# Attention heads of a two-block model handled by the pair, and head norms of its recurrence taken per token, on one Trainium2 core

## What is computed

```
kk = heads(k * k_k)
kk = kk / jnp.maximum(jnp.sqrt(jnp.sum(kk * kk, axis=-1, keepdims=True)), 1e-12)
...
mean = jnp.mean(wkv, axis=-1, keepdims=True)
var = jnp.mean(jnp.square(wkv - mean), axis=-1, keepdims=True)
y = ((wkv - mean) * lax.rsqrt(var + GN_EPS)) * ln_w + ln_b
```

```
s = jnp.einsum('bqgrd,bkgd->bgrqk', qi, k).astype(jnp.float32) * scale
p = jax.nn.softmax(s, axis=-1).astype(v.dtype)
return jnp.einsum('bgrqk,bkgv->bqgrv', p, v)
```

## Time and profile before

| | |
|---|---|
| median of 3 runs | 2863.81 us (2863.75 to 2866.16) |
| profiled execution | 2862.11 us, of which the span is 2860.3 us |
| mean granted clock of TensorE | 0.966 |
| PE busy | 2600.9 us (91%) |
| DVE, ACT, POOL busy | 1240.2, 1085.9, 809.8 us (43, 38, 28%) |
| heads, layer 1 | from 2123.5 to 2335.6 us of the span |
| heads, layer 2 | from 2624.9 to 2789.5 us |
| rounds | from 471.2 to 1052.1 us |

### The profile page before, as it was taken

The page is one execution under the profiler, slowest core; times in us unless marked ns, Lnnn a source line. Parts: engine busy times, 40 slices in busy tenths (PEclk is TensorE's granted clock), DMA queues, the critical chain, the costliest instruction groups (busy, mean ns, idle before and its releaser), DMA issues. The chain is left out here.

```text
span 2860.3 us, 49221 instructions
## 1 busy us (share of the span) xinstructions
PE 2600.9 (91%) x19266; PEld 2041.7 (71%) x19266; DVE 1240.2 (43%) x1839; ACT 1085.9 (38%) x1682; POOL 809.8 (28%) x342
## 2 busy tenths in 40 slices
PE   8999979989898979888999999989978888998987
PEld 6887857868686857776778887767855566776665
DVE  3222024455655537344242220055846642584652
ACT  4443224343434323553233442233344422335441
POOL 3444433313232313112434444412210002232002
PEclk9999989999999989999999999999999999999998
DMA  4232322212121212111423233311110001121001
GB/s 135 90 95 92 105 66 86 91 52 83 59 83 59 83 39 74 52 38 59 134 82 95 88 95 98 100 37 53 55 41 1 1 9 51 52 74 59 1 1 66
DMA packets 52005, 188.49 MB, mean 66 GB/s; under 512 B 5760, under 2 KB 6016, under 8 KB 51712
## 3 DMA queue, kind: packets, MB, share of 16 engines
q1 hardware_dynamic: 50688, 181.74, 20.3%
q10 hardware_dynamic: 1152, 4.26, 0.4%
HBM read 183.88 MB, written 2.10 MB: 65 GB/s over the span
## 5 line engine op out<-in xcount | busy, mean ns | idle before, releaser
L2392 POOL TENSOR_TENSOR WLO<-RAW,WHI 128x1024 fp32r<-128x1024 f32 x334 | 804.7, 2409 | 2010.5 <-ACT WHI L299 2010.5
L299 ACT ACTIVATE WHI<-RAW 128x1024 fp32r<-128x1024 f32 x336 | 355.8, 1059 | 999.7 <-PE psum L313 708.8
L311 PE MATMUL psum<-HHI,WHI 128*128 128x512 f32 x872 | 353.8, 406 | 40.2 <-DVE HLO L397 15.0
L312 PE MATMUL psum<-HLO,WHI 128*128 128x512 f32 x872 | 347.0, 398 | 0.0
L313 PE MATMUL psum<-HHI,WLO 128*128 128x512 f32 x872 | 346.6, 397 | 0.0
L311 PE MATMUL psum<-H2HI,WHI 128*128 128x512 f32 (+1 forms) x536 | 197.3, 368 | 32.5 <-DVE H2LO L395 23.0
L311 PEld LDWEIGHTS psum<-HHI,WHI 128*128 128x128 f32 x872 | 165.8, 190 | 84.0 <-issue 43.9
L312 PEld LDWEIGHTS psum<-HLO,WHI 128*128 128x128 f32 x872 | 165.9, 190 | 41.7 <-issue 3.4
L313 PEld LDWEIGHTS psum<-HHI,WLO 128*128 128x128 f32 x872 | 165.7, 190 | 39.6
L312 PE MATMUL psum<-H2LO,WHI 128*128 128x512 f32 (+1 forms) x536 | 191.6, 357 | 0.0
L313 PE MATMUL psum<-H2HI,WLO 128*128 128x512 f32 (+1 forms) x536 | 191.2, 357 | 0.0
(11 more groups left out here) (394 smaller groups left out, 5196.6 us busy)
## 6 DMA issues: line engine op xcount, KB each, us to landing
RAW<-in_wstream SPq DMA_DIRECT2D x336, 512.0 KB, 3.5
X<-in_xT SPq DMA_DIRECT2D x8, 256.0 KB, 7.3
out_T<-OUT SPq DMA_DIRECT2D x4, 512.0 KB, 2.6
W3S<-in_lora ACTq DMA_DIRECT2D x5, 384.0 KB, 3.1
XC<-in_ctxT ACTq DMA_DIRECT2D x1, 1024.0 KB, 5.6
TRIG<-in_trig ACTq DMA_DIRECT2D x1, 960.0 KB, 7.6
FCC<-in_first SPq DMA_DIRECT2D x1, 576.0 KB, 9.0
LVL<-in_levels SPq DMA_DIRECT2D x1, 384.0 KB, 9.3
```

What stands on the lines that cost most here:

```text
L299: act.activation(WHI[:, q % 2, :], RAW[:, q % 2, :], ACT.Copy).then_inc(rounded, 1)
L311: pe.matmul(out, tile_of(WHI, slot, u), hi(kt), start=first and last[0], stop=False)
L312: pe.matmul(out, tile_of(WHI, slot, u), lo(kt), start=False, stop=False)
L2392: pool.tensor_tensor(WLO[:, s, :], RAW[:, s, :], WHI[:, s, :].bitcast(F32), ALU.subtract)\
```

## The change

**Heads.** A pair's two units are handled together. PE's order per pair becomes: transposes of both units (`trl`, `trh`: first 512 columns, then 256), the scores of both units of the next pair (`scl`, `sch`), then the values. Maximum (`mxl`, `mxh`) and exponentials (`exl`, `exh`) are taken in two pieces of 512 and 256 columns with one small step to join the two maxima and one (`dn`) to add the two sums. The inverses are taken once per pair. GQA scores are issued in pieces of 256 columns, in turn for a = 0 and a = 1. `lo` comes one pair later.

**Rounds.** The head sums of `kkss` and `var` are taken with the operands swapped (`token_sums`): tokens on partitions, 8 columns per pair of heads. Root, maximum and reciprocal work on these 8 columns (`ROOT`), and a new PE step (`spread`: `kkb` after `streamed(1)`, `varb` after the last piece of `streamed(5)`) puts the result back on the channels, in PSUM. `low_ranks` waits for `n0`, since `varb` and it use the same bank; `e3` no longer waits for `kk`.

```diff
--- before.py
+++ after.py
+        ROOT = ra("ROOT", [P, 2, 2 * BLOCKS])
...
+                def token_sums(name, p, src, *waits):
+                    for w in waits:
+                        pe.wait_ge(*w)
+                    for b in range(BLOCKS):
+                        mm = pe.matmul(SETS[p].B[0][:, 2 * b:2 * b + 2], src[:, b * P:(b + 1) * P], two_heads, start=True, stop=True)
+                    mm.then_inc(*S.inc(f"{name}_{p}"))
...
+                def spread(name, p, *waits):
+                    for w in waits:
+                        pe.wait_ge(*w)
+                    pe.sem_inc(tensor_ready)
+                    for b in range(BLOCKS):
+                        for h in range(2):
+                            mm = pe.matmul(SETS[p].B[0][h * HD:(h + 1) * HD, b * P:(b + 1) * P],
+                                           ROOT[:, p, 2 * b + h:2 * b + h + 1].to_broadcast([P, HD]), eye, start=True, stop=True)
+                    mm.then_inc(*S.inc(f"{name}_{p}"))
...
-                    pe.wait_ge(*A.before(f"sd_{p}", i))
-                    pe.wait_ge(*V.before(f"dd_{p}", i))
+                    pe.wait_ge(*V.before(f"n0_{p}", i))
...
-                    head_sums("kkss", p, SETS[p].B[0], SETS[p].E1[:, :], A.at(f"kksq_{p}", i))
-                whole(streamed(1), streamed(2))
+                    token_sums("kkss", p, SETS[p].E1, A.at(f"kksq_{p}", i))
+                whole(streamed(1))
+                for p in TWO:
+                    spread("kkb", p, V.at(f"kkinv_{p}", i))
+                whole(streamed(2))
                 head_sums("bonus", 0, SETS[0].B[1], SETS[0].RK[:, :], V.at("rk_0", i))
...
-                    head_sums("var", p, SETS[p].B[0], SETS[p].DSQ[:, :], A.at(f"dsq_{p}", i))
+                    token_sums("var", p, SETS[p].DSQ, A.at(f"dsq_{p}", i))
                 whole(tail)
+                for p in TWO:
+                    spread("varb", p, V.at(f"rinv_{p}", i))
...
-                    run("e3", p, d.E3[:, :], d.SG[:, :], ACT.Exp, V.at(f"cprev_{p}", i), V.at(f"kk_{p}", i), scale=-DECAY)
+                    run("e3", p, d.E3[:, :], d.SG[:, :], ACT.Exp, V.at(f"cprev_{p}", i), scale=-DECAY)
...
-                    run("kkn", p, d.E3[:, :], d.B[0], ACT.Sqrt, S.at(f"kkss_{p}", i))
+                    run("kkn", p, ROOT[:, p, :], d.B[0][:, 0:2 * BLOCKS], ACT.Sqrt, S.at(f"kkss_{p}", i))
...
-                    run("sd", p, SETS[p].E1[:, :], SETS[p].B[0], ACT.Sqrt, S.at(f"var_{p}", i), scale=1.0 / HD, bias=EPS[:, 1:2])
+                    run("sd", p, ROOT[:, p, :], SETS[p].B[0][:, 0:2 * BLOCKS], ACT.Sqrt, S.at(f"var_{p}", i), scale=1.0 / HD, bias=EPS[:, 1:2])
...
+                def unit_root(p):
+                    ts(f"kkmax_{p}", ROOT[:, p, :], ROOT[:, p, :], 1e-12, None, ALU.max, None, A.at(f"kkn_{p}", i))
+                    inverse(f"kkinv_{p}", ROOT[:, p, :], V.at(f"kkmax_{p}", i))
                 def unit_key(p):
                     d = SETS[p]
-                    ts(f"kkmax_{p}", d.E3[:, :], d.E3[:, :], 1e-12, None, ALU.max, None, A.at(f"kkn_{p}", i))
-                    inverse(f"kkinv_{p}", d.E3[:, :], V.at(f"kkmax_{p}", i))
-                    stt(f"kk_{p}", d.KK[:, :], d.RKV[:, 1, :], col("k_k", i * 2 + p), d.E3[:, :], ALU.mult, ALU.mult, V.at(f"kkinv_{p}", i))
+                    stt(f"kk_{p}", d.KK[:, :], d.RKV[:, 1, :], col("k_k", i * 2 + p), d.B[0], ALU.mult, ALU.mult, S.at(f"kkb_{p}", i))
...
+                unit_root(0)
+                unit_root(1)
...
+                    inverse(f"rinv_{p}", ROOT[:, p, :], A.at(f"sd_{p}", i))
+                for p in TWO:
                     d = SETS[p]
                     dv = d.DV[:, :]
-                    inverse(f"rinv_{p}", d.E1[:, :], A.at(f"sd_{p}", i))
-                    tt(f"n0_{p}", dv, dv, d.E1[:, :], ALU.mult, V.at(f"rinv_{p}", i))
+                    tt(f"n0_{p}", dv, dv, d.B[0], ALU.mult, S.at(f"varb_{p}", i))
...
-        COLS = 4 * KB
+        COLS = 2 * KB
+        SCORES, TURNED = two_banks[0:2], two_banks[2:4]
+        VALUES = two_banks[3][:, TT:TT + 2 * P]
...
+            def scores(j):
+                kind, i, _, qb = us[2 * j]
+                low = qb < BLOCKS
+                qs = slice(qb * P, (qb + 1) * P)
                 pe.sem_inc(tensor_ready)
-                hs = slice(a * HD, a * HD + HD)
-                qs = slice(qb * P, (qb + 1) * P)
-                for at, w in ((0, T), (T, TC)):
-                    if qb >= BLOCKS and not at:
-                        continue
-                    lhs, rhs = ((QAM[:, i * 2 + a, qs], KAM[:, i * 2 + a, at:at + w]) if kind == "mla" else
-                                (QAG[hs, i, qs], KAG[hs, at:at + w]))
-                    mm = pe.matmul(two_banks[a][:, at:at + w], lhs, rhs, start=True, stop=True)
-                mm.then_inc(*S.inc(f"sc{u}"))
+                if kind == "mla":
+                    for a in range(2):
+                        for z, at, w in (("l", 0, T), ("h", T, TC)):
+                            if low or at:
+                                pe.matmul(SCORES[a][:, at:at + w], QAM[:, i * 2 + a, qs], KAM[:, i * 2 + a, at:at + w], start=True, stop=True)\
+                                  .then_inc(*S.inc(f"sc{z}{2 * j + a}"))
+                else:
+                    for at in range(0 if low else T, TT, TC):
+                        for a in range(2):
+                            hs = slice(a * HD, a * HD + HD)
+                            mm = pe.matmul(SCORES[a][:, at:at + TC], QAG[hs, i, qs], KAG[hs, at:at + TC], start=True, stop=True)
+                            if at + TC in (T, TT):
+                                mm.then_inc(*S.inc(f"sc{'l' if at < T else 'h'}{2 * j + a}"))
...
+            def turned(j):
+                low = us[2 * j][3] < BLOCKS
+                for a in range(2):
+                    u = 2 * j + a
+                    for z, bs in (("l", range(BLOCKS)), ("h", range(BLOCKS, KB))):
+                        if z == "l" and not low:
+                            continue
+                        pe.wait_ge(*A.at(f"ex{z}{u}"))
+                        if j and a and z == "h":
+                            pe.wait_ge(*V.at(f"y{j - 1}"))
+                        pe.sem_inc(tensor_ready)
+                        for b in bs:
+                            mm = pe.transpose(TURNED[a][:, b * P:(b + 1) * P], PX[:, a, b * P:(b + 1) * P], eye)
+                        mm.then_inc(*S.inc(f"tr{z}{u}"))
...
+                pe.wait_ge(*V.at(f"pt{2 * j + 1}"))
+                if qb < BLOCKS:
+                    pe.wait_ge(*A.at(f"pt{2 * j + 1}"))
...
+            for j in range(n):
+                turned(j)
+                if j + 1 < n:
+                    scores(j + 1)
+                values(j)
...
+            def exponent(u):
+                kind, _, a, qb = us[u]
+                act.wait_ge(*V.at(f"nm{u}"))
+                if u >= 2:
+                    act.wait_ge(*S.at(f"trh{u - 2}"))
+                for z, c, cols in (("l", slice(0, T), part_cols(u)[0]), ("h", slice(T, TT), part_cols(u)[1])):
+                    if z == "h" or qb < BLOCKS:
+                        act.activation(PX[:, a, c], SCORES[a][:, c], ACT.Exp, scale=scale_of(kind), bias=NM2[:, u % COLS:u % COLS + 1],
+                                       accum_out=DEN2[:, cols]).then_inc(*A.inc(f"ex{z}{u}"))
...
+            for j in range(n):
+                for a in range(2):
+                    exponent(2 * j + a)
+                if us[2 * j][3] < BLOCKS:
+                    for a in range(2):
+                        act.wait_ge(*S.at(f"trl{2 * j + a}"))
+                        if j:
+                            act.wait_ge(*S.at(f"pv{j - 1}"))
+                        act.activation(PTS[:, a, 0:T], TURNED[a][:, 0:T], ACT.Copy).then_inc(*A.inc(f"pt{2 * j + a}"))
                     rounded_part(j - 1)
...
+                lo, hi = part_cols(u)
+                nm = NM2[:, u % COLS:u % COLS + 1]
+                for z, c, cols in (("l", slice(0, T), lo), ("h", slice(T, TT), hi)):
+                    if z == "h" or qb < BLOCKS:
+                        dve.wait_ge(*S.at(f"sc{z}{u}"))
+                        dve.tensor_reduce(MX2[:, cols], SCORES[a][:, c], AX, ALU.max).then_inc(*V.inc(f"mx{z}{u}"))
+                dve.wait_ge(*V.at(f"mxh{u}"))
+                if qb < BLOCKS:
+                    dve.tensor_scalar(nm, MX2[:, lo], MX2[:, hi], -scale_of(kind), ALU.max, ALU.mult).then_inc(*V.inc(f"nm{u}"))
+                else:
+                    dve.tensor_scalar(nm, MX2[:, hi], -scale_of(kind), None, ALU.mult).then_inc(*V.inc(f"nm{u}"))
+            def inverse(j):
+                c, h = 2 * j % COLS, COLS + 2 * j % COLS
+                dve.wait_ge(*A.at(f"exh{2 * j + 1}"))
+                if us[2 * j][3] < BLOCKS:
+                    dve.tensor_tensor(DEN2[:, c:c + 2], DEN2[:, c:c + 2], DEN2[:, h:h + 2], ALU.add).then_inc(*V.inc(f"dn{j}"))
+                    dve.wait_ge(*V.at(f"dn{j}"))
```

(20 more changed lines are left out.)

134 lines of the change are left out of this document (41 added, 93 removed).

## The result

| | before | after |
|---|---|---|
| median of the runs, us | 2863.8 (4 runs, 2854.6 to 2866.2) | 2772.7 (4 runs, 2767.3 to 2778.8) |
| profiled execution, its span, us | 2862.1, 2860.3 | 2775.5, 2773.7 |
| end of the rounds (first PE product behind them), us | 1052.10 | 1028.14 |
| heads stage of layer 1, first scores to first product behind it, us | 212.1 | 176.9 |
| heads stage of layer 2, us | 164.6 | 140.0 |

The ratio is 0.9699, with a 95% interval of 0.9683 to 0.9716: 91 us faster by the medians (86 by the ratio), where 65 were forecast. By the two traces 86.6 us of span went: 59.8 in the heads' stages and 24.0 up to the end of the rounds. Another 4.2 went behind layer 2's heads, which nothing in the change touches, and 1.2 came back between the two heads stages.

A forecast was written before the change was run, and what follows sets the result against it. PE, busy 91% of the span, was taken as the bound. Heads -50 and rounds -15 took the profiled 2862.1 us to 2797, plus 1.7 for the median: 2799 us; range 2781 (nearly -58 and -22) to 2829.

The forecast's parts named there:

- The MLA pair: Heads, low MLA pair: PE's own work is the bound, 5.7 us per pair in place of 6.44.
- The high pairs: Heads of layer 1, twelve steps: 3.1 us each in place of 4.2.
- 5.6 per GQA pair: Heads, low GQA pair: the DVE and ACT chain decides, 5.6 us per pair, a gain of 0.86.
- end 5.41, plus the switch of 0.1 to 0.2: Heads: chain of a low pair from its scores' start through maxima, exponentials and last transposes, 5.41 us, plus a switch.
- The same seven us or so: Heads, first pair before the windows: takes about seven us as before, since both units' scores come first.
- The boundary: Turn from one round to the next: `bonus_0` 2.3 us earlier, 3.9 with KTOK's wait gone; three boundaries -12.
- The new wait before `kkb`: Round boundary: PE waits 2.3 us for `kkinv_0` before `kkb`, with `streamed(2)` queued behind it.
- `low_ranks(0)` at 610.7: Round boundary: first low-rank products start at 610.7 us on the trace, against 608.82 before.
- A: Heads: GQA scores don't overlap on row halves; 11 us of the gain lost, 2810 us; chance 0.12.
- B: Heads: a pair's chain is longer, 6.0 to 6.2 us for all low pairs; 2819 us; chance 0.14.
- C: Rounds give nothing, as the wait before `kkb` lets the clock fall; 2814 us; chance 0.11.
- D: Heads: the clock falls with PE's lower share of GQA pairs, slower than before; 2898 us; chance 0.03.

The follow-up runs named there:

- e4: The changed kernel with grouped scores issued unit 0 whole, then unit 1 whole, in the same pieces of 256 columns; 2772.8 us, ratio 0.9688.
- e12: The changed kernel with grouped scores issued unit 0 whole, then unit 1 whole, in the old pieces of 512 and 256 columns; 2773.1 us, ratio 0.9685.
- e6: The changed kernel with `spread` of `varb` moved ahead of the last two steps of the tail block; 2771.3 us, ratio 0.9678.
- e11: The kernel before with 48 idle semaphore instructions on PE ahead of the squared keys' sums; 2858.6 us, ratio 0.9994.
- e3: The kernel before with 96 idle semaphore instructions on PE ahead of the squared keys' sums; 2873.8 us, ratio 1.0039.
- e8: The changed kernel with the squared keys' norm as before, the token form kept only for `var`; 2782.9 us, ratio 0.9726.
- e1: The kernel before with the heads' part of the change alone; 2798.7 us, ratio 0.9771.
- e7: The changed kernel with all three remaining steps of the tail block behind the `spread` of `varb`; 2766.0 us, ratio 0.9670.
- e9: The kernel of e7 with DVE's `mod_sum` and `mods` moved ahead of the means' differences; 2757.4 us, ratio 0.9641.

## Why the prediction was wrong, step by step

**Heads, windows: -57.6 for -50.** The MLA pair is right, 5.72 for 5.7 and PE-bound. The high pairs are right: twelve steps of layer 1 go from one low MLA pair to the same place 57.0 us later (2121.82 to 2178.82), 57.0 - 4 x 5.72 - 4 x 5.37 = 12.7, so 3.2 each for 3.1, as a mean with the switches between groups in it. What failed is the term "5.6 per GQA pair": it is 5.37, 24 times 0.23, 5.5 us. The step was the chain's sum "end 5.41, plus the switch of 0.1 to 0.2". Its head was right with the switch (first maximum 1.17 behind the scores' start). But the maxima repeat in 1.19, not 1.29, since the negative overlaps what follows; and the pieces of the exponentials start 0.68 apart, not 0.77, because the next one starts while the accumulator of the one before is still being read (2146.64 against 2146.54 + 0.19). Each hand-off had been taken whole from a row where nothing could overlap it. Of the rest 1.6 are in layer 2, where the equal steps of the sum missed the switches: MLA to GQA takes 4.6, three times, GQA to MLA 6.5, twice, and the last period is 4.55.

**Outside the windows: 2.2 for nothing.** "The same seven us or so" ahead of the first pair was right in that little changes (10.8 to 10.5 in layer 1), and wrong in the size. The rest is a shorter way out, 2.92 to 2.64 and 5.17 to 3.81 from the last `pv`. Most of the 1.4 in layer 2 is clock: in before it was at half for 3.4 us from 2783.7 on, and there the row of values took 2.66 us, in after 1.51.

**Rounds: -24.0 for -15.** The boundary was forecast at -3.9 with every landmark placed: with its mean's products laid on those of before (5.04 later), after's first boundary puts `low_ranks(0)` at 612.4 (forecast 610.7), the end of DVE's products at 616.4 (616.7), `kkss` at 623.8 (623.0), `kkb` at 632.5 (632.9) and `bonus_0` at 640.1 (640.4). Three of them gave 10.5 for 12, the end 4.4 for 4.0. `token_sums` started 16 products in 1.70 (618.78 to 620.48), 0.85 a pair for 0.96, and `spread` 0.06 a record as taken. The new wait before `kkb` is 1.2 in the first boundary and under 0.4 in the other two, for 2.3, since PE itself comes later there: the jump costs 1.5 more ("`low_ranks(0)` at 610.7" had carried the loop's turn over at its old 1.1, though the long products that covered it now stand ahead of `spread`), and in two of three the clock fell behind it.

The step that failed here is one that the forecast did not have: a stretch without any edit, the state steps, was carried over at its old length. The records added ahead of it moved the packets of instructions against the state steps and PE's stop out of them, and with the stops (4.7) went the stretch at half clock behind the first. Those 8.5 us are nearly the whole difference to 24.0. The forecast had the 1.10 of the loop's turn in its rows, and stops of the same kind, 0.91 to 1.73 in every round's state steps, stood in the same trace unused.

**Together:** 7.6 in the heads' windows, 2.2 around them, 9 in the rounds and 2.8 net elsewhere, where no code was changed, make the 21.6 of the span. The medians of the runs give 26, since the profiled execution of before lies 1.7 below its median and that of after 2.8 above its own. No single term takes the time out of the range: with the 8.5 alone the forecast would have been 2790, with the 5.5 of the GQA pairs as well 2785. The range itself had little room below: -58 and -22 give 2784, not 2781. The mechanism of the heads holds; in the rounds it holds for the boundaries and missed the state steps.

**The rivals.** A fell: twelve score records take 1.50, not 2.98 (e4 and e12 overlap too). B fell: periods went below the forecast, not above. C's condition, a low clock behind the new wait, did not come in the first boundary, where the wait was (PEclk 1.00 from 600 to 630). In the others the clock fell behind the jump. C's mechanism can occur all the same: in e6, where the wait before `kkb` was 1.83 and 1.16 in one boundary and 4.06 in the next, the clock fell behind it; behind the 1.20 of after and the 1.00 of e6's third boundary it did not. D fell: the clock stayed at 1.00 in both windows, though by the Trainium skill's rule on transposes (TensorE: Matmul & The Clock Gate, Part 4: PE-mode transpose) a GQA pair shows the gate 3.2 of 5.37 us; no run here shows an effect of it.

## What to carry to other kernels

Add up a chain with the spacing of starts (start to start of repeated steps), not with durations plus a hand-off each: where two steps of one engine follow, part of the hand-off lies under the next. Before costing an edit that adds or removes many short instructions, list the places where the engine stops for "issue", see whether instruction packets land 1 to 2 us before, and count the instructions ahead; the stops can move with the count, onto short products (where they cost) or long ones (where they don't). Keep a few long products between the last wait of a loop's body and its jump, and put small steps that others wait for at the end into an idle stretch before, away from POOL's passes.

## What the runs showed of the hardware that was not expected

- PE's stops without a wait stand at places that the number of instructions ahead sets: 48 or 96 idle ones ahead took a stop of 0.9 to 1.7 us out of the same step in all rounds (e11, e3), undoing one half of an edit brought it back (e8). Its size varies from 0.25 to 1.83 at one place (e8, e1). Each of 32 such stops ends 1.25 to 1.60 us after a packet of 16384 bytes on the instruction queue has landed (all 14 traces).
- The jump to a loop's start costs PE 2.5 to 3.0 us where 32 short records stand ahead of it, 0.95 to 1.24 with nine long ones between (e7), and none to 0.68 in e9, whose PE code is that of e7. The first products behind it start 1.71 to 2.00 us after such a packet (all 14 traces); the packets took 0.93 to 0.98 us in e9 and 1.22 to 1.41 in e7.
- Instructions that only raise a semaphore are not free on PE: 96 of them delayed the next product by 10.6 us (e3), 48 by 3.3 (e11, round 1), so the cost does not grow in proportion.
- Products on the two row halves overlap fully when four records of one half stand ahead of four of the other, and in part with six ahead of six, 2.03 for 1.50 (e12, e4).
- Records of 2 columns, each with a whole load of weights, start 0.106 us apart (1.70 / 16, after).
- A POOL pass held an 8-column `tensor_scalar` on DVE for 2.09 and 2.35 us in place of 0.16, and not the 8-column reciprocal ahead of the first of them (e6).
